# A gated recurrent stage by thirds of the tokens, its convolution deferred, its output made with tokens on partitions

## The reference

```
proj = h @ w_in
cb, cc, ch, q, k, v, g, lr = jnp.split(proj, IN_SPLITS, axis=-1)
uc, new_buf = short_conv(cc * ch, conv_buf, conv_w)
y_conv = cb * uc
log_a = jax.nn.log_sigmoid((lr @ gate_up + gate_b).astype(jnp.float32)) / GLA_TAU
o, s_new = gla_chunked(q, k, v, log_a, s0)      # recurrent over chunks of 64 tokens, 4 heads
o = rmsnorm(o, gla_g.reshape(GLA_HEADS, GLA_DV)).reshape(Bn, T, GLA_V)
y_gla = (o * jax.nn.silu(g.astype(jnp.float32))).astype(h.dtype)
y = jnp.concatenate([y_conv, y_gla], axis=-1) @ w_out
```

## Time and profile before

| | us |
|---|---|
| median of 3 runs | 1161.9 |
| lowest and highest run | 1159.37, 1163.62 |
| the profiled execution, device time | 1160.94 |
| its span, first to last instruction | 1159.0 |
| TensorE busy in the span | 1088.7 |
| VectorE, ScalarE busy | 433.3, 357.4 |
| the chain that ended last, share of TensorE | 82% |

### The profile page before, as it was taken

One profiled execution on the slowest core, in us unless ns is written; L12 is line 12 of the kernel. 1 busy time (PEld: TensorE's weight loads), 2 busy tenths in 40 slices (PEclk: granted clock), 3 DMA queues, 4 the chain that ended last, 5 costly groups with the idle time before them and its releaser, 6 DMA issues.

```text
span 1159.0 us, 13739 instructions
## 1 busy us (share of the span) xinstructions
PE 1088.7 (94%) x5732; PEld 850.8 (73%) x5732; DVE 433.3 (37%) x718; ACT 357.4 (31%) x566; POOL 95.1 (8%) x108
## 2 busy tenths in 40 slices
PE   7999999899999899899999989899997799999995
PEld 6788988789889779688799978678886544444442
DVE  6824501426352542633333363433227311222222
ACT  6726512111111103422121156522111111445453
POOL 1000000000000000000000000000000222344443
PEclk9998999889998998899999999999996799999998
DMA  9572201001110311532164462344325789787831
GB/s 363 168 169 73 55 1 37 19 19 37 37 29 28 78 55 44 174 110 82 66 201 146 153 249 91 133 140 160 113 101 230 288 358 365 286 353 288 326 106 53
DMA packets 88407, 167.48 MB, mean 144 GB/s; under 512 B 19026, under 2 KB 60306, under 8 KB 81428
## 3 DMA queue, kind: packets, MB, share of 16 engines
q1 hardware_dynamic: 75380, 141.15, 34.5%
q0 software_dynamic: 12960, 25.39, 6.2%
HBM read 145.05 MB, written 43.29 MB: 163 GB/s over the span
## 4 chain that ended last, share of the span: by engine, by line
PE 82%; DVE 8%; ACT 5%; issue 2%; DMA 1%; POOL 0%; POOLq 0%; SPq 0%; DVEq 0%; ACTq 0%
PE G L1401 14%; PE G L1319 11%; PE G L1321 11%; PE G L1320 11%; PE G L795 10%; PE G L817 4%; PE G L799 2%; PE T L1593 2%; PE T L787 2%; PE T L1418 2%; PE G L822 1%; PE T L1589 1%; PE G L1449 1%; PE T L1636 1%; PE G L1658 1%
## 5 line engine op out<-in xcount | busy, mean ns | idle before, releaser
L1319 PE MATMUL G<-act_hi,w_hi 128*128 128x344 f32 x672 | 228.2, 340 | 15.5 <-DVE arena L2040 4.9
L1320 PE MATMUL G<-act_lo,w_hi 128*128 128x344 f32 x672 | 221.0, 329 | 0.0
L1321 PE MATMUL G<-act_hi,w_lo 128*128 128x344 f32 x672 | 220.7, 328 | 0.0
L1319 PEld LDWEIGHTS G<-act_hi,w_hi 128*128 128x128 f32 x672 | 132.1, 197 | 26.2 <-issue 21.8
L1401 PE MATMUL G<-wt,act_hi 128*128 128x512 f32 x512 | 143.5, 403 | 5.3 <-DVE act_lo L2252 4.9
L1320 PEld LDWEIGHTS G<-act_lo,w_hi 128*128 128x128 f32 x672 | 132.1, 197 | 1.5 <-issue 1.4
L1321 PEld LDWEIGHTS G<-act_hi,w_lo 128*128 128x128 f32 x672 | 131.8, 196 | 0.0
L1401 PEld LDWEIGHTS G<-wt,act_hi 128*128 128x128 f32 x512 | 96.5, 191 | 28.4 <-issue 5.6
L795 PE MATMUL G<-wring,misc 128*128 128x512 f32 x256 | 114.3, 600 | 1.2 <-ACT misc L864 1.2
L687 POOL DMA_INDIRECT misc<-d_h,tidx x20 | 20.5, 1025 | 955.1 <-DVE tidx L1008 896.4
L795 PEld LDWEIGHTS G<-wring,misc 128*128 128x128 f32 x256 | 48.2, 193 | 56.2 <-issue 56.2
(11 more groups left out here) (358 smaller groups left out, 1528.5 us busy)
## 6 DMA issues: line engine op xcount, KB each, us to landing
wring<-in_w_gate_dram SPq DMA_DIRECT2D x16, 1024.0 KB, 11.3
wring<-in_w_up_dram SPq DMA_DIRECT2D x16, 1024.0 KB, 13.9
wring<-in_w_down_dram SPq DMA_DIRECT2D x16, 1024.0 KB, 16.9
arena<-in_w_in_dram SPq DMA_DIRECT2D x24, 512.0 KB, 3.9
arena<-in_x_prompt_dram SPq DMA_DIRECT2D x16, 512.0 KB, 7.1
d_x<-arena SPq DMA_DIRECT2D x16, 512.0 KB
arena<-in_cache_mem_k_dram SPq DMA_DIRECT2D x8, 1024.0 KB, 5.5
arena<-in_w_k_dram SPq DMA_DIRECT2D x8, 512.0 KB, 6.3
```

Of the source, the lines that this page charges most:

```text
L1319: pe.matmul(out, a_hi, b_hi, start=first, stop=False)
L1320: pe.matmul(out, a_hi, b_lo, start=False, stop=False)
L1321: return pe.matmul(out, a_lo, b_hi, start=False, stop=last)
```

## The change

Each block of the stage is now made by thirds of the columns: the column third is the outer loop and k the inner one, 24 matmuls a third, and each third signals (`th_done`) and is read by itself (`third_out`). A third of a block waits only until the same third of the block before it is read (`wait_third`). The step list puts one recurrent step ahead of each third instead of ahead of each part.

The convolution (`conv`) stands in VectorE's order behind the first third of `cb`, and thus behind the step ahead of that third, where it stood directly behind the reading of `ch`.

`go` makes the recurrent output with tokens on partitions: the masked scores are the weights and the values the 128 columns; q's 64 tokens of a chunk are the weights (64 x 64) and the state the 128 columns. The norm of a head is then a sum along a row: four ScalarE squares with a row sum, a root and a VectorE reciprocal of four columns, a product. A new step `gt` (four transposes on TensorE, a ScalarE copy) brings the result back to features on partitions; it stands behind the next tile's `gd`. The step `gm` is gone. The next tile's `ga` now waits for the product (`a_norm`), where it waited for ScalarE's two reads (`a_sq`).

Of the stage's result each third is cast and subtracted (`ys`) behind its own third of the last block. Three weight blocks of the projection are split ahead of the last block, one behind its first third, four at the end; before, four were split ahead of its reading and four at the end. The projection's first token tile waits for the last third's reading and its own third of the result.

```diff
     for t in range(NT):
-        steps += [[("ga", t), ("gk", t)], [("gd", t)], [("go", t)], [("gm", t)]]
-    PARTS = ((0, 3), (3, 6), (6, KB))
+        steps += [[("ga", t), ("gk", t)], [("gd", t)] + [("gt", t - 1)] * (t >= 1), [("go", t)], []]
...
-    for n in range(at[("cc", 0)], at[("g", VB - 1)] + 1):
+    for n in GLA:
+        kind, b = kinds[n]
         order.append(("begin", n))
-        for part in PARTS:
+        if n == GLA[-1]:
+            order += [("split", at[("out", k)]) for k in range(3)]
+        for c in range(NCH):
             if steps:
                 order += steps.pop(0)
-            order.append(("part", (n, part)))
...
+            order.append(("part", (n, c)))
+            if kind == "cb" and c == 0:
+                order.append(("conv", b))
+            order.append(("ev", (n, c)))
+            if n == GLA[-1]:
+                order += [("yg", 0)] * (c == NCH - 1) + [("ys", c)] + [("split", at[("out", 3)])] * (c == 0)
...
+        def wait_third(eng, n, c):
+
+            mine = ("cc", "g") if kinds[n][0] in ("cc", "g") else ("ch", "cb")
+            eng.wait_ge(s["tf_a" if mine[0] == "cc" else "tf_d"], NCH * len([m for m in GLA if m < n and kinds[m][0] in mine]) + c + 1)
...
+            def gla_part(n, c):
+
+                j, slot = gla[n], nth[n] % 2
+                if c == 0:
+                    pe.wait_ge(s["split_done"], n + 1)
+                if j >= 1:
+                    wait_third(pe, GLA[j - 1], c)
+                elif c == 0:
+                    pe.wait_ge(s["vt_ev"], TILES - 1)
+                for k in range(KB):
+                    ins = mm3(gla_at[:, c, 0:CH], w_hi[:, slot, k, :], w_lo[:, slot, k, :],
+                              act_hi[:, k, third(c)], act_lo[:, k, third(c)], k == 0, k == KB - 1)
+                ins.then_inc(s["th_done"], 1)
...
+                if stage == 1 and 0 < t < NT and k0 == 0:
+                    pe.wait_ge(s["ys_lo"], 3 * ((c0 + r - 1) // CH + 1))
...
-                            pe.wait_ge(s["ys_lo"], k + 1)
+                            pe.wait_ge(s["ys_lo"], 1 if k < CB else 2 if k < KB - 1 else 3)
...
-                        pe.wait_ge(s["a_sq"], t)
+                        pe.wait_ge(s["a_norm"], t)
...
-                    for q in range(2):
-                        for k in range(QB):
-                            h = 2 * k + q
-                            pe.matmul(T[:, q, k * P:(k + 1) * P], vtm[:, t, h * DV:(h + 1) * DV], Am[t % 2][:, q, k, :],
-                                      start=True, stop=False)
-                            for c in range(2):
-                                a0 = k * P + c * CHUNK
-                                ins = pe.matmul(T[:, q, a0:a0 + CHUNK], S[q * DK:(q + 1) * DK, (2 * t + c) % 4, k, :],
-                                                qe[q * DK:(q + 1) * DK, k, c0 + c * CHUNK:c0 + (c + 1) * CHUNK],
-                                                start=False, stop=(c == 1))
+                    for h in (0, 2, 1, 3):
+                        q, k = h % 2, h // 2
+                        pe.matmul(heads_out[:, q, k, :], Am[t % 2][:, q, k, :], vtm[:, t, h * DV:(h + 1) * DV], start=True, stop=False)
+                        for c in range(2):
+                            ins = pe.matmul(heads_out[c * CHUNK:(c + 1) * CHUNK, q, k, :],
+                                            qe[q * DK:(q + 1) * DK, k, c0 + c * CHUNK:c0 + (c + 1) * CHUNK],
+                                            S[q * DK:(q + 1) * DK, (2 * t + c) % 4, k, :], start=False, stop=True)
                     ins.then_inc(s["a_o"], 1)
-                elif what == "gm":
-                    pe.wait_ge(s["a_sq"], i + 1)
-                    pe.matmul(X[:, 0, :], ones[:, :], gsq[:, :], start=True, stop=True).then_inc(s["a_ms"], 1)
+                elif what == "gt":
+                    pe.wait_ge(s["a_norm"], i + 1)
+                    pe.wait_ge(s["a_kdt"], min(i + 2, NT))
+                    for h in range(HEADS):
+                        ins = pe.transpose(X[:, 0, h * P:(h + 1) * P], on[:, h % 2, h // 2, :], ident[:, :])
+                    ins.then_inc(s["a_gt"], 1)
...
-                    act.copy(feat[:, 0:VB, t * P:(t + 1) * P].rearrange("p (k q) n -> p q k n", q=2), lower4)
-                    act.activation(gsq.rearrange("p (q n) -> p q n", q=2), T[:, :, 0:QB * P], ACT.Square).then_inc(s["a_sq"], 1)
...
+                    for h in range(HEADS):
+                        ins = act.activation(grt[:, h * DV:(h + 1) * DV], heads_out[:, h // QB, h % QB, :], ACT.Square, accum_out=gst[:, h:h + 1])
+                    link(ins)
+                    act.activation(gst[:, HEADS:2 * HEADS], gst[:, 0:HEADS], ACT.Sqrt, scale=1.0 / DV, bias=epsb[:, 0:1]).then_inc(s["a_rt"], 1)
+                elif what == "gt":
+                    act.wait_ge(s["a_gt"], i + 1)
+                    act.copy(feat[:, 0:VB, i * P:(i + 1) * P], X[:, 0, :].rearrange("p (h n) -> p h n", h=HEADS)).then_inc(s["a_ev"], 1)
...
-                    link(v.reciprocal(grt[:, :], grt[:, :]))
...
+                    link(v.reciprocal(gst[:, 2 * HEADS:3 * HEADS], gst[:, HEADS:2 * HEADS]))
+                    if t >= 1:
+                        dve.wait_ge(s["a_gt"], t)
+                    v.tensor_tensor(on, heads_out, bcast(gst[:, 2 * HEADS:3 * HEADS].rearrange("p (q k) -> p q k", q=2).unsqueeze(3),
+                                                         [P, 2, QB, DV]), ALU.mult).then_inc(s["a_norm"], 1)
...
+                elif what == "ys":
+                    for p, (a, b, f) in enumerate(((0, CB, VB), (CB, KB - 1, 0), (KB - 1, KB, VB - 1))):
+                        dve.wait_ge(s["ys_hi"], 3 * i + p + 1)
+                        v.tensor_tensor(act_lo[:, a:b, third(i)], feat[:, f:f + b - a, third(i)], act_hi[:, a:b, third(i)],
+                                        ALU.subtract).then_inc(s["ys_lo"], 1)
```

More of the change, by code:

```diff
@@ L116, in use_z, with big @@
         return nth[Z0] + i
+    GLA = list(range(at[("cc", 0)], at[("g", VB - 1)] + 1))
+    gla = {n: j for j, n in enumerate(GLA)}
+    gla_uses = [use(n) for n in GLA]
     grp, cnt = [], []
     for u in range(NCOL + QB):
-        beside_gla = use(at[("cc", 0)]) <= u <= use(at[("g", VB - 1)])
-        g = 0 if beside_gla else (1 - grp[-1] if grp else 1)
-        cnt.append(grp.count(g))
+        g = 0 if u in gla_uses else (1 - grp[-1] if grp else 1)
+        cnt.append(len([x for x in range(u) if grp[x] == g and x not in gla_uses]))
         grp.append(g)
+    def big(u):
+        return len([x for x in range(u + 1) if x not in gla_uses])
     order = [("mem", t) for t in range(MB)]
@@ L182, in token_stage @@
         return seq
-    order += [("ysplit", 0)] + [("split", at[("out", k)]) for k in range(KB // 2, KB)]
+    order += [("ysplit", 0)] + [("split", at[("out", k)]) for k in range(4, KB)]
     order += token_stage(1)
@@ L436, in wait_free, with third @@
             for g in range(2):
-                eng.wait_ge(free[g], grp[:use(n) + 1].count(g))
+                eng.wait_ge(free[g], len([u for u in range(use(n) + 1) if grp[u] == g and u not in gla_uses]))
+        def wait_third(eng, n, c):
+            mine = ("cc", "g") if kinds[n][0] in ("cc", "g") else ("ch", "cb")
+            eng.wait_ge(s["tf_a" if mine[0] == "cc" else "tf_d"], NCH * len([m for m in GLA if m < n and kinds[m][0] in mine]) + c + 1)
+        def third(c):
+            return slice(c * CH, (c + 1) * CH)
         links = {}
@@ L2134, in _ @@
                         late(behind.pop(0))
-                    if what != "begin":
-                        read_out(i)
                 elif what == "fw0":
@@ L2241, in _ @@
                     link(v.tensor_tensor(o3, o3, grt[:, 0:n].rearrange("p (q k b) -> p q k b", q=2, k=QB), ALU.mult))
-                elif what == "ysplit":
-                    dve.wait_ge(s["g_used"], VB)
+                elif what == "ev":
+                    third_out(*i)
+                elif what == "conv":
+                    conv(i)
+                elif what == "yg":
+                    dve.wait_ge(s["g_used"], NCH * VB)
                     for h in range(VB):
```

233 lines of the change are left out of this document (118 added, 115 removed).

## The result

The changed kernel takes 1114.96 us in the median of 4 runs (1112.98 to 1116.7), the kernel before 1160.63 in 4 runs beside it: a ratio of 0.961, 95% interval 0.9585 to 0.963, 45.7 us less. Forecast were 1119 us, 42 us less.

What follows compares the result with a forecast made beforehand. TensorE, busy for 94% of the span, was taken to bound the kernel. Idle time 18.4, output piece 7.5 and clock 11.1 + 5 made 42.0 us off 1160.94: 1119 us, range 1111 to 1136 us.

Steps and rivals of the forecast that it cites:

- Thirds: At the stage's block boundaries, TensorE's waits for readings of the accumulator go entirely: 12.4 us.
- Convolution deferred: State updates now stand ahead of the convolution in VectorE's queue, so TensorE's wait for the recurrent state goes: 2.5 us.
- Sample states: TensorE's wait of 1.6 us for the sample states stays and grows by 0.8 us.
- Split of the result: At the start of the projection, the wait for the stage's split result falls from 4.9 to 0.6 us.
- The output piece: Each tile's four-head recurrent output on TensorE shrinks from 3.91 to 3.0 us: 7.5 us over 8 tiles.
- The rival in which it keeps its length: The output piece stays at 3.9 us as its weight loads cannot overlap: 1131 to 1132 us; chance 0.20.
- Sum of squares against transposes: Per tile, a 0.45 us matmul of ones goes and four transposes of 0.40 us come: no difference.
- The clock: In stage and projection, falls of TensorE's granted clock go: 11.1 us behind standstills, 5 us of 6.4 behind long output pieces.
- with the standstill goes the fall: Four clock falls behind TensorE standstills, of 4.6, 1.7, 1.5 and 3.3 us, vanish with those waits: 11.1 us.
- VectorE's queue: Rival: convolution and splits ahead of the readings keep the banks, half the idle and clock gains return: 1134 us; chance 0.07.
- the transposes: Rival: each tile's state update and transposes pull the clock down, eight falls of 1.6 us: 1130 us; chance 0.05.
- the normalisation's chain: Slower rival: squares, root, reciprocal and product, some 3.9 us, outlast their 7.6 us cover of two thirds: 1167 us; chance 0.04.

Runs made afterwards that it cites:

- whole_blocks: The changed kernel with the matmuls of a block in the old order, the next block waiting for all three banks, readings still in thirds: 1124.38 us.
- conv_at_once: The changed kernel with the convolution directly behind the reading of block ch in VectorE's order, no longer behind the next third: 1120.58 us.
- paired_later: The changed kernel with output-piece heads paired on the two row halves and one more third of matmuls ahead of the sample output, kept whole: 1099.6 us.
- late_split: The changed kernel with the stage's result cast and subtracted as before, all after the last block: 1120.84 us.
- slow_chain: The changed kernel with twenty extra, discarded ScalarE squares in each tile's normalisation, between row sums and root: 1125.4 us.
- old_output: The changed kernel with the recurrent output and its normalisation made as before (features on partitions, sum of squares by matmul), thirds kept: 1133.05 us.

## Why the prediction was right, step by step

*Thirds, 12.4 us.* Right: between the blocks no reading of the accumulator stands among the releasers any more. The convolution in front of the first third of `cb`, the one doubt, cost nothing. What whole_blocks adds is that the order of the matmuls alone is worth 4.4 us of this, and that the early split rests on it.

*Convolution deferred, 2.5 us.* Right, by conv_at_once: 2.7 us at the tile named.

*Sample states, 0.8 us more.* Right in size (2.2 us against the 2.4 forecast). What I missed is that more than its own 2.2 us goes with it, 3.0 to 5.3 us by paired_later.

*Split of the result, 4.9 to 0.6 us.* Right to the tenth; late_split has a wait of 3.7 us there again. No wait for the eighth weight block shows.

*The output piece, 3.0 us.* 3.03. The rival in which it keeps its length falls. The term itself, 7.5 us, is 7.3 by its own figures (8 x 0.91), and 7.0 was measured.

*Sum of squares against transposes, nothing.* Wrong, 3.2 us. The step took the 0.45 us to the start of the next matmul for the whole price, and the stretch behind paid 0.36 us more, which the trace of before showed.

*The clock, 16.1 us.* The sum is near (17.5, or 16.7 by the granted clock), the reasons are borne out in part. The step "with the standstill goes the fall" named four falls. The two dearest are borne out: that behind the state wait, 4.6 us (conv_at_once: 0.29 of 11.68 us, 3.4), and that at the projection, 3.3 us (late_split: 3.0). The other two, 1.7 and 1.5 us behind block boundaries, went with their waits, but no run brings them back alone. The waits ahead of them were 2.4 and 3.4 us, the longest of L2056 and L2040 in the earlier trace rows; those that leave the clock at 1.00 are shorter, up to 1.7 us in whole_blocks and 2.3 in slow_chain. The long output piece was not near: from the end of the stretch behind the last one to the end of the wait, the clock in before is 1.00.

```profile
232.55:239.76 7.21, 4.85 (x32) 3.83 (x31) 5.33 (x4) 2.03 (x3) 0.00 (x0) 1.00 0.00 0
376.99:384.20 7.21, 3.83 (x22) 3.10 (x21) 5.30 (x4) 1.74 (x2) 0.00 (x0) 1.00 0.00 0
```

Of the long pieces, four of eight take the clock down with no wait at all, by 7.7 us in old_output's four stretches, and the piece of 3.03 us did so nowhere in the changed kernel, so all of the 6.4 us came back that I counted as 5. That "the long fall round the sample output stays" was not right: it grew by 1.7 us.

*The rivals.* VectorE's queue keeps no bank; the transposes pull nothing down, even threefold; the normalisation's chain has a cover of two thirds, as worked out, and it took 6.2 us more a tile to cost 10 us in all. That the chain's 3.9 us of the forecast meet the first tile's 3.8 is luck: its squares follow each other 0.26 us apart and not 0.46, and 1.28 us are a table load that the sum did not have. Where the time lies that the forecast missed: 3.2 us in the sum of squares, 1.4 in the clock, 1.5 outside the stage, 0.3 in the idle time, less 0.5 at the piece.

Not settled: the four parts undone one by one give back 18 + 9.4 + 5.9 + 5.6 = 39 us of the 45.7. The rest would lie in what all four kept, the readings in thirds above all (of the 12.4 us of boundary waits whole_blocks brought back 4.4); they were not undone by themselves.

## What to carry to other kernels

Price a small matmul by two windows, to the start of the next one and over the stretch behind it. Where small matmuls use half the rows of the array, put two that use different halves side by side, which also saves changes of shape: together that was worth more here (8.7 us) than the shorter output piece of the new layout (7.0 us). And ask of each fall of the clock whether the piece alone, the wait alone, or both together make it, since taking away a wait ahead of a piece that takes the clock down can give back more than its length (3.0 to 5.3 us for 2.2 here). And look at more than one execution, since a fall of the same piece is not always as long.

## What the runs showed of the hardware that I had not expected

A float matmul with 512 moving columns delayed the stretch behind it by 0.36 to 0.39 us beyond the 0.45 us to the start of the next one; four transposes did not (209.81 to 213.69: 24 matmuls in 3.88 us, as behind an output piece). Eight matmuls with 64 x 64 weights on both row halves took the 0.37 us of four on one. The sample output's matmuls of one column were followed by a fall of the clock in three of four pieces of 1.87 us, with no wait ahead, while the changed kernel's output pieces of 3.03 us were followed by none; with a wait of 2.7 us ahead, one was (conv_at_once). And the root's table load of 1.28 us on ScalarE comes at the first tile only: the squares and copies between the later roots bring no other, and the next is at the first silu, behind the last tile.
